# The inverse of the delta rule's triangular blocks: one matrix kept and turned by TensorE, in place of a matrix and its transpose carried by two products

## What is computed

```
q, k, v, g, beta = (chunk(t) for t in (q, k, v, g, beta))      # chunks of 64 tokens
g = jnp.cumsum(g, axis=-1)
decay = jnp.exp(jnp.where(lower, g[..., :, None] - g[..., None, :], -jnp.inf))
kk = jnp.einsum('bnhcd,bnhed->bnhce', k, k)
lmat = jnp.where(strict, beta[..., :, None] * kk * decay, 0.0)
amat = lmat + jnp.eye(DN_CHUNK, dtype=lmat.dtype)
rhs = jnp.concatenate([v * beta[..., None], k * (beta * jnp.exp(g))[..., None]], axis=-1)
sol = lax.linalg.triangular_solve(amat, rhs, left_side=True, lower=True, unit_diagonal=True)
```

## Time and profile before

| | us |
|---|---|
| three timed runs | 3394.2, 3397.3, 3403.93 |
| their median | 3397.3 |
| the profiled execution, first to last instruction (span) | 3393.1 |
| PE busy | 3195.2 (94%) |
| DVE busy | 2324.7 (69%) |
| ACT busy | 1601.3 (47%) |
| POOL busy | 111.8 (3%) |
| levels 0 to 5, layer 0 | 263.7 to 321.2 |
| levels 0 to 5, layer 1 | 914.6 to 972.0 |

### The profile page before, as it was taken

The page is one execution under the profiler, slowest core; times in us unless marked ns, Lnnn a source line. Parts: engine busy times, 40 slices in busy tenths (PEclk is TensorE's granted clock), DMA queues, the critical chain, the costliest instruction groups (busy, mean ns, idle before and its releaser), DMA issues.

```text
span 3393.1 us, 51194 instructions
## 1 busy us (share of the span) xinstructions
PE 3195.2 (94%) x20700; PEld 2862.5 (84%) x20700; DVE 2324.7 (69%) x2592; ACT 1601.3 (47%) x1572; POOL 111.8 (3%) x118
## 2 busy tenths in 40 slices
PE   6999999999998799999999999899569999998999
PEld 6999899999997688788788888799348998996799
DVE  7976388846762488788788888499884443547344
ACT  3444143435441377677677777343114323435333
POOL 0004000000220000000000000000000000000000
PEclk8999999989999899999999999999789999999999
DMA  8640288635203299999999999355105543541253
GB/s 324 258 151 1 105 304 309 260 113 179 93 13 112 73 360 374 335 365 368 333 367 369 368 368 366 135 184 185 38 25 190 183 161 124 198 163 36 87 185 125
DMA packets 129898, 703.21 MB, mean 207 GB/s; under 512 B 11040, under 2 KB 15408, under 8 KB 73904
## 3 DMA queue, kind: packets, MB, share of 16 engines
q1 hardware_dynamic: 118672, 650.30, 52.6%
q0 software_dynamic: 6880, 48.24, 3.6%
q10 hardware_dynamic: 4160, 2.12, 0.2%
HBM read 698.50 MB, written 1.07 MB: 206 GB/s over the span
## 4 chain that ended last, share of the span: by engine, by line
PE 57%; DVE 5%; ACT 2%; issue 1%; DMA 0%; PEld 0%; SPq 0%; ACTq 0%; DVEq 0%; PEldq 0%
PE banks L482 16%; PE banks L483 16%; PE banks L484 16%; PE banks L430 3%; DVE big L1213 2%; PE banks L978 1%; PE banks L443 1%; PE banks L787 1%; PE banks L1037 1%; DVE tail L1213 0%; DVE tail L1232 0%; PE banks L1074 0%; DVE big L1930 0%; DMA ring<-in_wall 0%; DVE ring_low L1213 0%
## 5 line engine op out<-in xcount | busy, mean ns | idle before, releaser
L1213 DVE TENSOR_TENSOR ring_low<-ring,parts 128x2048 fp32r<-128x2048 f32 x570 | 1297.1, 2288 | 378.5 <-ACT parts L2137 358.7
L482 PE MATMUL banks<-parts 128*128 128x256 f32 (+1 forms) x3712 | 1170.0, 315 | 37.3 <-DVE tail_parts L1213 18.4
L483 PE MATMUL banks<-tail_parts,parts 128*128 128x256 f32 x3744 | 1061.7, 284 | 0.0
L2137 ACT ACTIVATE parts<-ring 128x2048 fp32r<-128x2048 f32 x234 | 448.5, 1917 | 815.9 <-PE banks L484 714.6
L484 PE MATMUL banks<-parts,ring_low 128*128 128x256 f32 x2816 | 797.5, 283 | 0.0
L482 PEld LDWEIGHTS banks<-parts 128*128 128x128 f32 x3712 | 707.6, 191 | 79.8 <-issue 38.9
L2210 ACT ACTIVATE parts<-ring 128x2048 fp32r<-128x2048 f32 x336 | 644.4, 1918 | 225.3 <-DMA ring<-in_wall 207.2
L483 PEld LDWEIGHTS banks<-tail_parts,parts 128*128 128x128 f32 x3744 | 711.8, 190 | 1.9 <-issue 1.9
L484 PEld LDWEIGHTS banks<-parts,ring_low 128*128 128x128 f32 x2816 | 537.2, 191 | 0.0
L483 PE MATMUL banks<-ring_low,parts 128*128 128x512 f32 x896 | 354.7, 396 | 0.0
L484 PE MATMUL banks<-parts,tail_parts 128*128 128x512 f32 x896 | 353.1, 394 | 0.0
(11 more groups left out here) (418 smaller groups left out, 3571.0 us busy)
## 6 DMA issues: line engine op xcount, KB each, us to landing
ring<-in_wall SPq DMA_DIRECT2D x616, 1024.0 KB, 6.2
big<-in_wall POOLq DMA_DIRECT2D x40, 1024.0 KB, 5.5
big<-in_w_k POOLq DMA_DIRECT2D x1, 2048.0 KB, 9.3
big<-in_w_v POOLq DMA_DIRECT2D x1, 2048.0 KB, 17.6
big<-bias_table ACTq DMA_DIRECT2D x2, 1024.0 KB, 7.6
constants<-in_con SPq DMA_DIRECT2D x1, 1249.5 KB, 8.7
x<-in_x SPq DMA_DIRECT2D x1, 1024.0 KB, 6.4
big<-big POOLq DMA_DIRECT2D x16, 64.0 KB, 4.9
```

What stands on the lines that cost most here:

```text
L482: pe.matmul(o, high, in_high, start=start, stop=False, **kw)
L483: pe.matmul(o, high, in_low, start=False, stop=False, **kw)
L1213: return ve.tensor_tensor(out, a, b, op)
L2137: act(parts(w_high(room, n), UNIT), ring[n % RING][:, :], ACT.Copy).then_inc(sem("w_high"), 1)
```

## The change

In levels 0 to 4 only the inverse E is carried. After U of a group PE turns E of that group (four transposes into bank 4 + q % 2), ACT copies the turned block to F, and the one product of the group is F-transposed times U, subtracted from E. Level 5 turns E too, and makes U-transposed times F, subtracted from F, as before. `first_turned` and `first_out` go. DVE's subtraction raises level_t itself. POOL's program stays, apart from the count of lt_out.

```
-                first_turned(0)
                 for s in range(6):
                     for q in range(4):
-                        if s == 0 and q < 3:
-                            first_turned(q + 1)
                         pe.wait_ge(*at("level_mask", 4 * s + q + 1, l, 24))
                         if s:
                             pe.wait_ge(*at("level_t", 4 * (s - 1) + q + 1, l, 24))
                         else:
-                            pe.wait_ge(*at("lt_out", 5 + q, l, 8))
+                            pe.wait_ge(*at("level_init", q + 1, l, 4))
+                            pe.wait_ge(*at("qk_out", q + 1, l, 4))
                         for c in range(4):
...
                         mm.then_inc(sem("level_u"), 1)
+                        if 4 * s + q >= 2:
+                            pe.wait_ge(*at("level_f", 4 * s + q - 1, l, 24))
+                        for c in range(4):
+                            mm = pe.transpose(bank[4 + q % 2][:, c * P:(c + 1) * P], block(SLOT["E"], q, c), ident)
+                        mm.then_inc(sem("level_turned"), 1)
                     for q in range(4):
                         pe.wait_ge(*at("level_uc", 4 * s + q + 1, l, 24))
+                        pe.wait_ge(*at("level_f", 4 * s + q + 1, l, 24))
                         if 4 * s + q >= 2:
                             pe.wait_ge(*at("level_t", 4 * s + q - 1, l, 24))
                         for c in range(4):
-                            x = (4 * q + c) * P
-                            if s < 5:
-                                pe.matmul(bank[4 + q % 2][:, c * P:(c + 1) * P], big(SLOT["F"] + x, P), big(UBUF + x, P),
-                                          start=True, stop=True)
-                            mm = pe.matmul(bank[6 + q % 2][:, c * P:(c + 1) * P], big(UBUF + x, P),
-                                           big(SLOT["F"] + x, P), start=True, stop=True)
+                            inverse_t, u = block(SLOT["F"], q, c), block(UBUF, q, c)
+                            if s == 5:
+                                inverse_t, u = u, inverse_t
+                            mm = pe.matmul(bank[6 + q % 2][:, c * P:(c + 1) * P], inverse_t, u, start=True, stop=True)
                         mm.then_inc(sem("level_p"), 1)
...
                         ve.wait_ge(*at("level_p", 4 * s + q + 1, l, 24))
-                        x = q * 512
-                        if s < 5:
-                            tt(big(SLOT["E"] + x, 512), big(SLOT["E"] + x, 512), bank[4 + q % 2][:, :], ALU.subtract)
-                        lk(tt(big(SLOT["F"] + x, 512), big(SLOT["F"] + x, 512), bank[6 + q % 2][:, :], ALU.subtract))
-                        ve.nop().then_inc(sem("level_t"), 1)
+                        inverse = big(SLOT["E" if s < 5 else "F"] + q * 512, 512)
+                        tt(inverse, inverse, bank[6 + q % 2][:, :], ALU.subtract).then_inc(sem("level_t"), 1)
...
-                        if s == 0 and q < 3:
-                            first_out(q + 1)
                         se.wait_ge(*at("level_u", 4 * s + q + 1, l, 24))
                         act(big(UBUF + q * 512, 512), bank[q][:, :], ACT.Copy).then_inc(sem("level_uc"), 1)
+                        se.wait_ge(*at("level_turned", 4 * s + q + 1, l, 24))
+                        act(big(SLOT["F"] + q * 512, 512), bank[4 + q % 2][:, :], ACT.Copy).then_inc(sem("level_f"), 1)
```

More of the change, by code:

```diff
@@ L556, in delta, with block @@
                     mm.then_inc(sem("lt"), 1)
[L558 to L564, removed]
-                first_turned(0)
+                def block(off, q, c):
+                    return big(off + (4 * q + c) * P, P)
                 for s in range(6):
                     for q in range(4):
-                        if s == 0 and q < 3:
-                            first_turned(q + 1)
                         pe.wait_ge(*at("level_mask", 4 * s + q + 1, l, 24))
@@ L575, in delta @@
                         else:
-                            pe.wait_ge(*at("lt_out", 5 + q, l, 8))
+                            pe.wait_ge(*at("level_init", q + 1, l, 4))
+                            pe.wait_ge(*at("qk_out", q + 1, l, 4))
                         for c in range(4):
-                            x = (4 * q + c) * P
-                            mm = pe.matmul(bank[q][:, c * P:(c + 1) * P], big(LTS + x, P), big(SLOT["E"] + x, P),
+                            mm = pe.matmul(bank[q][:, c * P:(c + 1) * P], block(LTS, q, c), block(SLOT["E"], q, c),
                                            start=True, stop=True)
                         mm.then_inc(sem("level_u"), 1)
+                        if 4 * s + q >= 2:
[3 more added lines that the diff above has]
+                        mm.then_inc(sem("level_turned"), 1)
                     for q in range(4):
                         pe.wait_ge(*at("level_uc", 4 * s + q + 1, l, 24))
+                        pe.wait_ge(*at("level_f", 4 * s + q + 1, l, 24))
                         if 4 * s + q >= 2:
@@ L2338, in _ @@
                 for b in range(4):
-                    se.wait_ge(*at("lt", b + 1, l, 8))
+                    se.wait_ge(*at("lt", b + 1, l, 4))
                     act(big(SLOT["C"] + b * 512, 512), bank[4 + b][:, :], ACT.Copy).then_inc(sem("lt_out"), 1)
[L2342 to L2347, removed]
                 for s in range(6):
                     for q in range(4):
-                        if s == 0 and q < 3:
-                            first_out(q + 1)
                         se.wait_ge(*at("level_u", 4 * s + q + 1, l, 24))
                         act(big(UBUF + q * 512, 512), bank[q][:, :], ACT.Copy).then_inc(sem("level_uc"), 1)
+                        se.wait_ge(*at("level_turned", 4 * s + q + 1, l, 24))
+                        act(big(SLOT["F"] + q * 512, 512), bank[4 + q % 2][:, :], ACT.Copy).then_inc(sem("level_f"), 1)
                     if s == 1:
@@ L2558, in _ @@
                         else:
-                            po.wait_ge(*at("lt_out", q + 1, l, 8))
+                            po.wait_ge(*at("lt_out", q + 1, l, 4))
                         po.tensor_tensor(view(BIG, LTS + q * 512, [[P, 4], [1, P]]), view(BIG, SLOT["C"] + q * 512, [[P, 4], [1, P]]),
```

## The result

The changed kernel took 3381.61 us (median of 4 runs, 3378.66 to 3384.01) against 3400.19 us for the one before (4 runs, 3394.2 to 3403.93): a ratio of 0.9953, with a 95% interval of 0.9939 to 0.9967. Faster by 0.5%, 18.6 us, where 17.5 were forecast.

A forecast was written before the change was run, and what follows sets the result against it. PE's issue rate was taken to bound the levels. Terms -17.8 + 2.0 + 0.4 - 2.1 = -17.5 us took the span from 3393.1 to 3375.6; with 4.2 added, 3379.8 us, range 3372 to 3389, at 85%.

The forecast's parts named there:

- What bounds the levels: From level 0's first product to level 5's end, PE's issue rate alone sets the time, 0.2233 us a product.
- Products -17.9, transposes +9.0 us a layer: Levels: 80 products at 0.2233 us go, 80 more transposes at 0.112 us come; net 17.8 us saved in two layers.
- The third product's wait, +2.0 us: Levels 0 to 4: each third product waits for DVE's subtraction to free its bank; 1.0 us lost a layer.
- ACT behind level 1, +0.4 us: ACT's side work after level 1 delays level 2's copies; 0 to 0.7 us a layer, 0.2 taken.
- The start of level 0, -2.1 us: Ahead of level 0, PE has less left after DVE's last block; 1.1 us gained in layer 0, 1.0 in layer 1.
- the rival effect: Layer 1's start: earlier U lets POOL run beside DVE's last operation, 1.64 instead of 0.69 us; at worst 0.3 lost.
- Sum: Whole kernel: the four terms together give -17.5 us, span 3393.1 to 3375.6 us.
- The starting level of 3397.3: Old kernel's median of three timed runs, 4.2 us above the profiled span; the same 4.2 was added to the forecast.
- A: Levels: transposes count as idling and PE's clock falls to 1.2 GHz; at most 3479 us; 4%.
- C: Levels: transposes cost their whole 272 ns; 3405.4 us, or 3407.6 and over with a few late-copy waits; 1%.
- D: Levels: PE runs a transpose as a product, 0.2233 us, so adds and removals cancel; 3397.6 us; 1%.
- B: Levels: products wait once per level for a late turned copy, 10.8 us given back; 3390.6 us; 6%.

The follow-up runs named there:

- e1: Changed kernel with the dropped product of levels 0 to 4 put back, read by nobody; one timed run 3412.2 us.
- e2: Changed kernel with every group of four transposes issued twice into the same bank; one timed run 3397.93 us.
- e7: Changed kernel with 320 more transposes in a row behind level 5 in each layer, read by nobody; timed 3448.89 us.
- e3: Changed kernel with the products of levels 0 to 4 written into the bank whose U was just copied out; 3376.47 us, ratio 0.9932 to the old kernel.
- e4: Old kernel with level_t raised by DVE's subtraction itself, without the wait and nop; timed 3391.51 us.
- e5: Changed kernel with ACT's copy of each turned block made twice, one after the other; timed 3374.52 us.
- b1: Old kernel once more, unaltered, for a second profile; the old kernel's median over 9 runs is 3396.78 us.
- after: Changed kernel as first timed and profiled, against the old kernel; 3381.61 us, ratio 0.9953.
- a1: Changed kernel once more, unaltered, timed in five runs against the old kernel; 3379.01 us, ratio 0.9946.

## Why the prediction was right

- *What bounds the levels.* Right. Taking 80 products out and putting them back (e1) moves each stretch by what PE issues, less the wait they cover; ACT, DVE and POOL did not take over.
- *Products -17.9, transposes +9.0 us a layer.* The product's price held (e1). The transpose's was 0.109 us by e2 and e7 and not 0.112; of my 3.59 us for 32 only 3.5 are theirs, the rest is the gap to the matmuls behind them, which I took in. 160 of them make 0.4 us.
- *The third product's wait, +2.0 us.* 0.21 us a level, 5 levels, 2 layers: 2.1 us, near the value that I chose between 0 and 0.27. e3 shows that the bank is the cause, and e4 that the nop's part is 0.06 us, as assumed.
- *ACT behind level 1, +0.4 us.* 0. The first copy was 0.9 us late, as worked out (1.0), and the first reader that could have waited came 0.5 us after the bank was free. e5 shows the room: another copy per group costs 2.2 us a layer.
- *The start of level 0, -2.1 us.* The step was rough. By the profiles of the table, layer 0 went from 11.1 to 12.5 us to 10.2 to 11.5, layer 1 from 14.0 to 14.2 to 13.2, so about -0.7 and -0.9, -1.6 in all. The reason given was half right. PE's shorter tail is there: from DVE's last operation to the first product it fell from 2.45 to 1.5 us in layer 0 and from 3.4 to 1.5 in layer 1. But I had DVE's end fixed at its old place in layer 0, and it moves from execution to execution, whatever the kernel, with the number of its operations that fall beside POOL's masks. With four slowed the start takes 11.1 us before (first profile, e4) and 10.2 to 10.3 in the changed kernel (e1, e5, e7); with five slowed, 12.45 before (b1) and 11.4 in the changed kernel (after, a1, e3). So at an equal number the change gains 0.9 to 1.0 us in layer 0, near the 1.1 forecast, and the rest is chance. For layer 1 the prediction had the rival effect in: DVE's last operation is now slowed too (1.64 us in place of 0.69) and DVE ends 0.9 us later. It also named the clock. In all three profiles of before the clock is at 1.2 GHz ahead of layer 1's products, in the first one until 913.3, which is 2.1 of the 3.4 us of the tail; in all profiles of the changed kernel it stays at 1.00. By an estimate from these figures that is 1.1 us of the tail, so that the 0.9 us gained in layer 1 is about what the clock gave back, and the shorter tail alone only makes up for DVE's later end. Why the clock stays up there was not tested.
- *Sum.* -16.2 from the levels and -1.6 from the starts are -17.8 us; -17.5 were forecast, -18.6 and -17.8 timed. The levels gave 0.8 more than forecast (-15.4) and the starts 0.5 less, so the sum came this near in part by luck. The starting level of 3397.3 was less good: 4.2 us between span and median were taken for a constant, but only 1.8 are outside the span and the rest is chance.
- *Rivals.* A is out (e7, and the clock of 1.00 in the levels of every profile), C is out (e2), D is out (0.109 us beside 0.2233), B is out as the kernel stands (e5).

## What to carry to other kernels

Price an instruction on a busy engine by the distance of starts in a back-to-back run of it, not by its mean duration: here a transpose has 272 ns of the one and 109 of the other, and the sign of the change hangs on it. When two products serve only to keep a matrix and its transpose in step, one product, a transpose and a copy on an engine with room cost less here (0.109 for a transpose against 0.2233 us for the product that goes), as long as the copy's reader comes a group or two later; then look for the bank that the faster rhythm runs into, and write the result where the operand has just been read out. A gain of half a per cent is read from marks around the edited stretch, which repeat to 0.01 us here, while whole runs of one program differ by several us.

## What the runs showed of the hardware

- Float32 transposes alone, 352 in a row for 38.5 us, keep PE's clock at 2.4 GHz, at 0.109 us each, just under half of a 128x128 float32 product (0.2233).
- Executions of one program differ in where and how long PE's clock is at 1.2 GHz, in stretches that no edit touches, and their time goes with it: the same work took 579.2 to 579.5 us with 13.7 us of missing clock, 581.2 to 582.4 with 17.1.
- DVE's operation on two SBUF tensors takes 0.69 us alone and 1.64 to 1.75 beside POOL's. A pair of the two engines' operations takes 1.70 us, more than POOL's 1.24 alone and less than the 1.9 of both. With one operand in PSUM DVE keeps 0.69 beside POOL.
